# Second expansion of a two-block transformer kernel: 20 of 22 weight blocks by Strassen's scheme

## What is computed

```python
def swiglu(h, w_in, w_out):
    a, b = jnp.split(h @ w_in, 2, axis=-1)
    return (jax.nn.silu(a) * b) @ w_out

# in second_block, FFN_HIDDEN = 2816
h = rmsnorm(x, ffn_norm_pre[i]) * (1.0 + sc2) + sh2
y = swiglu(h, ffn_w_in[i], ffn_w_out[i])
x = x + g2 * rmsnorm(y, ffn_norm_post[i])
```

## Time and profile before

| | |
|---|---|
| median of 3 runs | 1345.88 us (1344.02 to 1346.18) |
| span of the profiled execution, first to last instruction | 1343.4 us |
| its own time | not listed; the runs' median is 2.5 us above the span |
| mean granted TensorE clock | 0.984 |
| busy: TensorE matmul | 1295.9 us, 96% |
| busy: weight loads | 1042.2 us, 78% |
| busy: VectorE, ScalarE, GpSimd | 544.9, 568.5, 591.2 us |
| chain that ended last, by engine | TensorE 85%, VectorE 6%, ScalarE 3%, DMA 3% |

### The profile page before, as it was taken

One profiled execution on the slowest core, in us unless ns is written; L12 is line 12 of the kernel. 1 busy time (PEld: TensorE's weight loads), 2 busy tenths in 40 slices (PEclk: granted clock), 3 DMA queues, 4 the chain that ended last, 5 costly groups with the idle time before them and its releaser, 6 DMA issues.

```text
span 1343.4 us, 17523 instructions
## 1 busy us (share of the span) xinstructions
PE 1295.9 (96%) x6464; PEld 1042.2 (78%) x6464; DVE 544.9 (41%) x1080; ACT 568.5 (42%) x938; POOL 591.2 (44%) x494
## 2 busy tenths in 40 slices
PE   7899999998989999999999899999899999999998
PEld 1688878677878888888888788667688888888886
DVE  2576652678436444443542352783520000001113
ACT  3713455767344322233323454785452323223232
POOL 0334332468043444444665733455224444445561
PEclk9999999999889999999999999899999999999999
DMA  9427557050243555554423411111202222222221
GB/s 393 179 77 270 187 172 142 1 189 1 73 178 125 199 200 196 187 187 157 157 94 99 162 64 69 56 30 61 91 32 97 98 105 105 95 94 94 94 94 63
DMA packets 27402, 166.77 MB, mean 124 GB/s; under 512 B 2976, under 2 KB 5280, under 8 KB 8656
## 3 DMA queue, kind: packets, MB, share of 16 engines
q1 hardware_dynamic: 25328, 151.31, 32.4%
q10 hardware_dynamic: 2016, 14.68, 2.9%
HBM read 163.85 MB, written 6.32 MB: 127 GB/s over the span
## 4 chain that ended last, share of the span: by engine, by line
PE 85%; DVE 6%; ACT 3%; DMA 3%; issue 1%; POOL 1%; SPq 0%; DVEq 0%; ACTq 0%
PE bank L275 55%; PE bank L334 12%; PE bank L311 6%; DMA ada_ring<-ada_dram 2%; DVE ada_ring L2018 1%; PE bank L1357 1%; PE bank L1329 1%; PE bank L714 1%; DMA w_raw<-w_dram 1%; PE bank L523 1%; DVE arena L2083 1%; PE bank L537 1%; PE bank L509 1%; PE bank L690 1%; POOL arena L942 1%
## 5 line engine op out<-in xcount | busy, mean ns | idle before, releaser
L268 POOL TENSOR_TENSOR w_lo<-w_raw,w_hi 128x512 fp32r<-128x512 f32 x328 | 444.0, 1385 | 620.2 <-ACT w_hi L259 620.2
L275 PE MATMUL bank<-h_hi,w_hi 128*128 128x512 f32 x1088 | 429.6, 395 | 7.4 <-DVE h_lo L450 4.5
L275 PE MATMUL bank<-h_lo,w_hi 128*128 128x512 f32 x1088 | 426.8, 392 | 0.0
L275 PE MATMUL bank<-h_hi,w_lo 128*128 128x512 f32 x1088 | 426.8, 392 | 0.0
L259 ACT ACTIVATE w_hi<-w_raw 128x2048 fp32r<-128x2048 f32 x86 | 164.8, 1917 | 309.0 <-PE bank L275 190.3
L275 PEld LDWEIGHTS bank<-h_hi,w_hi 128*128 128x128 f32 x1088 | 206.0, 189 | 51.4 <-issue 7.9
L275 PEld LDWEIGHTS bank<-h_hi,w_lo 128*128 128x128 f32 x1088 | 206.2, 190 | 43.5
L275 PEld LDWEIGHTS bank<-h_lo,w_hi 128*128 128x128 f32 x1088 | 206.4, 190 | 41.3
L2355 DVE TENSOR_TENSOR arena<-arena,bank 128x512 f32 (+1 forms) x22 | 15.1, 688 | 210.2 <-PE bank L275 210.2
L2211 DVE TENSOR_TENSOR h_lo<-arena,h_hi 128x1024 fp32r<-128x1024 f32 x22 | 32.4, 1485 | 135.1 <-ACT h_hi L1832 123.6
L2037 DVE SCALAR_TENSOR_TENSOR arena<-bank,params,arena 128x511 f32<-128x511 f32 (+1 forms) x36 | 25.3, 704 | 131.9 <-ACT arena L1807 111.6
(11 more groups left out here) (278 smaller groups left out, 1783.9 us busy)
## 6 DMA issues: line engine op xcount, KB each, us to landing
w_raw<-w_dram SPq DMA_DIRECT2D x92, 1024.0 KB, 4.7
ada_ring<-ada_dram SPq DMA_DIRECT2D x30, 1024.0 KB, 4.8
ada_ring<-ada_dram ACTq DMA_DIRECT2D x14, 1024.0 KB, 4.8
arena<-ada_dram SPq DMA_DIRECT2D x4, 1024.0 KB, 10.7
arena<-x_dram SPq DMA_DIRECT2D x2, 2048.0 KB, 11.5
bias_copies<-bias_rows SPq DMA_DIRECT2D x1, 4096.0 KB, 17.2
arena<-bias_copies SPq DMA_DIRECT2D x4, 768.0 KB, 5.7
ada_ring<-rpb_dram SPq DMA_DIRECT2D x16, 128.0 KB, 9.7
```

What stands on the lines that cost most here:

```text
L268: last = nc.gpsimd.tensor_tensor(w_lo[b % 2][:, part], w_raw[b % 2][:, part], w_hi[b % 2][:, part], ALU.subtract)
L275: last = nc.tensor.matmul(bank[:, :], w[:, ft, k, :], x[:, k, :], start=k == first and m == 0, stop=k == final and m == 2)
```

## The change

20 of the 22 expansion blocks, 61 to 80, are computed by Strassen's scheme in Winograd's form. A block is seen as a 2 x 2 matrix of quarters: inner dimension in halves of 4 chunks, output in gate and value tile. The activations are 2 x 2 as well: halves of the inner dimension by halves of the tokens (256 each). In place of 8 products of quarters there are 7, each 4 chunks x 3 matmuls with 256 moving columns, 84 matmuls in all.

- **Activation sums** (`h_sums`, four of 128x1024) are made once by VectorE after `h_lo`; ScalarE makes their high parts, VectorE two of the low parts and GpSimd two. `affine` keeps the full-precision activations in eight buffers (`h_full`).
- **Weight sums** (`w_sums`, four of 128x512) are made by VectorE for each block from `w_raw`.
- **Taking apart**: seven slots of 512 columns in the old `w_hi` and `w_lo` take the seven left operands. ScalarE makes seven copies of 512 columns (`high_slot`), GpSimd five subtractions and VectorE two (`low_slot`). A slot is refilled as soon as its product of the block before is done.
- **Putting together**: the seven products go to three banks (`PLACE`), two sets in turn. ScalarE copies products 0 and 4 out (`snapshot`), VectorE forms `left_gate` (512 columns), `third_sum`, `right_gate`, `left_value` (256 each, one input in a bank), GpSimd two 256-column sums from SBUF (`more_sums`). ScalarE's silu and VectorE's `gated2` now read SBUF alone.
- **Order**: TensorE's product 4 waits for the snapshot of product 0, product 5 for `third_sum`, product 6 for `left_gate`; a block waits for `gated2` of the block two before. The first contraction block is copied by ScalarE after product 3 of block 80 and is taken apart by GpSimd after `more_sums(19)`.
- The semaphores of the two attentions are merged and counted on by `of1`, which only renumbers waits.

```diff
+SEVEN0, SEVENS = B_UP2 + 2, 20
...
+        operand = [h_parts[0, 0], t_parts[1], h_parts[1, 0], t_parts[2], t_parts[0], h_parts[1, 1], t_parts[3]]
+        slot_part = [[w[1 - p // 4][:, p % 4 * 512:p % 4 * 512 + 512] for p in range(7)] for w in (w_hi, w_lo)]
+        seven_bank = [[ps[i] for i in (4, 5, 6)], [ps[i] for i in (1, 2, 3)]]
+        PLACE = [(0, 0), (1, 256), (1, 0), (2, 0), (0, 256), (2, 256), (1, 0)]
+        def slot_source(n, p):
+            return (raw_quarter(n, 0), w_sums[:, SUM2], raw_quarter(n, 1), w_sums[:, SUM3], w_sums[:, SUM1], w_sums[:, SUM4], raw_quarter(n, 3))[p]
...
@@ GpSimd
+            def low_slot(n, p, i=0):
+                pool.wait_ge(hi_done, HIGH0 + 7 * n + p + 1 + 14 * i)
+                nc.gpsimd.tensor_tensor(slot_part[1][p], slot_source(n, p), slot_part[0][p], ALU.subtract).then_inc(lo_done, 1)
+            def more_sums(n, i=0):
+                pool.wait_ge(seven_snap, 2 * n + 2 + 4 * i)
+                pool.wait_ge(seven_sum, 4 * n + 1 + 8 * i)
+                nc.gpsimd.tensor_tensor(u4[n % 2], gate_sum[n % 2][:, 256:512], p5_copy[n % 2], ALU.add).then_inc(seven_more, 1)
+                pool.wait_ge(seven_sum, 4 * n + 2 + 8 * i)
+                nc.gpsimd.tensor_tensor(value_sum[n % 2][:, 256:512], u3[n % 2], p5_copy[n % 2], ALU.add).then_inc(seven_more, 1)
+            def pool_turn(n, i=0):
+                for p in (0, 1, 2):
+                    low_slot(n + 1, p, i)
+                more_sums(n, i)
+                for p in (5, 6):
+                    low_slot(n + 1, p, i)
+            low_slot(0, 0)
+            low_slot(0, 1)
+            low_turned(2)
+            low_turned(0)
+            for p in (2, 5, 6):
+                low_slot(0, p)
...
@@ TensorE
+            def seven(n, i=0):
+                pe.wait_ge(tile_free, F_UP2 + 2 * n + 2 + 4 * i)
+                for p in range(7):
+                    if p in (3, 4):
+                        pe.wait_ge(seven_low, 2 + 2 * n + p - 2 + 4 * i)
+                    else:
+                        pe.wait_ge(lo_done, LOW0 + 5 * n + (p + 1 if p < 3 else p - 1) + 10 * i)
...
+                    if p == 4:
+                        pe.wait_ge(seven_snap, 2 * n + 1 + 4 * i)
+                    if p in (5, 6):
+                        pe.wait_ge(seven_sum, 4 * n + (2 if p == 5 else 1) + 8 * i)
+                    hi, lo = (slot_part[part][p].rearrange("p (k n) -> p k n", k=4) for part in range(2))
+                    out, (x_hi, x_lo) = product_at(n, p), operand[p]
+                    for k in range(4):
+                        for m, (w, x) in enumerate(((hi, x_hi), (hi, x_lo), (lo, x_hi))):
+                            last = nc.tensor.matmul(out, w[:, k], x[:, k], start=k == 0 and m == 0, stop=k == 3 and m == 2)
+                    last.then_inc(half_used, 1)
...
@@ ScalarE
+            def act_turn(n, i=0):
+                for p in range(7):
+                    if p == 0:
+                        snapshot(n, p, p1_copy, i)
+                    if p == 4:
+                        snapshot(n, p, p5_copy, i)
+                    if p == 6:
+                        gate_silu(n, i)
+                    high_slot(n + 1, p, i)
+            high_slot(0, 0)
+            for k, t in enumerate(TURNED):
+                act.wait_ge(t_sum, max(k, t) + 1)
+                nc.scalar.activation(t_parts[t][0], h_sums[:, t], ACT.Copy).then_inc(t_high, 1)
+            plain_silu(0)
...
+            act.wait_ge(half_used, USED0 + 7 * 19 + 4)
+            act.wait_ge(raw_in[1], 16 * (B_DOWN2 // 2 + 1))
+            nc.scalar.activation(w_hi[1][:], w_raw[1][:], ACT.Copy).then_inc(hi_done, 1)
+            snapshot(19, 4, p5_copy)
...
@@ VectorE
+            def weight_sums(n, i=0):
...
+                nc.vector.tensor_tensor(w_sums[:, SUM1], raw_quarter(n, 2), raw_quarter(n, 3), ALU.add).then_inc(w_sum, 1)
...
+                dve.wait_ge(w_sum, 4 * n + 1 + 8 * i)
+                nc.vector.tensor_tensor(w_sums[:, SUM2], w_sums[:, SUM1], raw_quarter(n, 0), ALU.subtract).then_inc(w_sum, 1)
+            def weight_sums_too(n, i=0):
+                nc.vector.tensor_tensor(w_sums[:, SUM3], raw_quarter(n, 0), raw_quarter(n, 2), ALU.subtract).then_inc(w_sum, 1)
...
+                nc.vector.tensor_tensor(w_sums[:, SUM4], raw_quarter(n, 1), w_sums[:, SUM2], ALU.subtract).then_inc(w_sum, 1)
...
+            def dve_turn(n, i=0):
+                if n:
+                    left_value(n - 1, i)
+                weight_sums(n + 1, i)
+                if n == 0:
+                    plain_gated(1)
+                else:
+                    gated2(n - 1, i)
+                weight_sums_too(n + 1, i)
+                left_gate(n, i)
+                third_sum(n, i)
+                low_slot(n + 1, 3, i)
+                low_slot(n + 1, 4, i)
+                right_gate(n, i)
```

More of the change, by code:

```diff
@@ L418, in spread, with affine @@
             return last
-        def affine(act, m, gain, shift, xn, hb, aside=None, turned=None):
+        def affine(act, m, gain, shift, xn, hb, aside=None, turned=None, slots=2):
             for c in range(DC):
@@ L429, in affine @@
                 nc.scalar.activation(h_hi[:, c, :], src, ACT.Identity, bias=shift(c), scale=gain(c))
[L430 removed]
+                if k >= 2 and slots == 2:
                     act.wait_ge(h_low, k - 1)
[L432 removed]
+                nc.scalar.activation(hb[:, c % slots, :], src, ACT.Identity, bias=shift(c),
                                      scale=gain(c)).then_inc(aff_done, 1)
@@ L1679, in _ @@
             lead_turned()
-            tiles(B_UP2 + 2, F_UP2 + 4, 9)
-            last_turn(B_UP2 + 20, F_UP2 + 40)
+            seven(0)
+            seven(1)
+            with pe.Fori(0, 9) as i:
+                seven(2, i)
+                seven(3, i)
             down_rows(B_DOWN2, 11, F_UP2 + 44)
@@ new lines, in plain_silu @@
+            def plain_silu(u):
+                act.wait_ge(half_used, 2 * B_UP2 + 2 * u + 1)
+                nc.scalar.activation(gate_sum[u], ps[2 * u][:, :], ACT.Silu).then_inc(tap_silu, 1)
+            high_slot(0, 0)
[3 more added lines that the diff above has]
+            plain_silu(0)
+            for p in (1, 2, 3):
+                high_slot(0, p)
@@ new lines, in _ @@
+            plain_silu(1)
+            for p in (4, 5, 6):
+                high_slot(0, p)
+            with act.Fori(0, 9) as i:
+                act_turn(0, i)
+                act_turn(1, i)
+            act_turn(18)
+            snapshot(19, 0, p1_copy)
+            for t in range(2):
+                nc.scalar.activation(h_hi[:, 2 * t:2 * t + 2, :], HID[:, 2 * t:2 * t + 2, :], ACT.Copy).then_inc(g_hi, 1)
+            act.wait_ge(half_used, USED0 + 7 * 19 + 4)
+            act.wait_ge(raw_in[1], 16 * (B_DOWN2 // 2 + 1))
@@ L2362, in _ @@
+            weight_sums(0)
+            turned_low(1)
+            weight_sums_too(0)
+            plain_gated(0)
+            turned_low(3)
+            low_slot(0, 3)
+            low_slot(0, 4)
+            dve_turn(0)
+            dve_turn(1)
+            with dve.Fori(0, 8) as i:
+                dve_turn(2, i)
+                dve_turn(3, i)
+            dve_turn(18)
+            left_value(18)
+            gated2(18)
             hidden_low(12, slice(0, 2), 0)
+            left_gate(19)
@@ L2363, in _ @@
+            third_sum(19)
             hidden_low(13, slice(2, 4), 2)
-            gated2(21)
+            right_gate(19)
+            left_value(19)
+            gated2(19)
             with dve.Fori(0, 3) as i:
```

198 lines of the change are left out of this document (149 added, 49 removed).

## The result

The kernel after takes 1407.39 us (median of 4 runs, 1406.23 to 1408.56), the one before 1345.81 (4 runs, 1344.02 to 1346.18): ratio 1.0463, 95% interval 1.0449 to 1.0478, 4.6% slower. The prediction was 1367.0, with a range of 1349 to 1382. The sign is right and the size is not: 61.6 us lost in place of 21.1. The profiled execution took 1407.43 us over a span of 1405.6, at a mean granted clock of 0.961.

A forecast was written before the change was run, and what follows sets the result against it. TensorE was taken to bound the kernel before, at 10.88 us a block. After: 19 x 11.6 = 220.4, + 2.5 + 15.1 + 0.7 = 238.7 us against 217.6, 21.1 slower; 1345.9 + 21.1 = 1367.0 us, range 1349 to 1382.

The forecast's parts named there:

- TensorE's own turn: 84 matmuls a block at 0.113 us, 9.52 us; as the bound it was a rival at 1325 us, chance 0.10.
- GpSimd and VectorE hold each other up: Two-SBUF-input VectorE operations and GpSimd's exclude each other: floor 10.9 us a turn; as the bound a rival, 1354 us, 0.18.
- The rival by which a VectorE operation is paid for whole: Both engines hold SBUF for their full duration, 0.69 in place of 0.45 us: turn 12.5, 1384 us, chance 0.08.
- VectorE's chain: Part of the turn from left_value through the weight sums, gated2 and left_gate to the end of third_sum.
- the good case: Second weight sum 0.7 us after the first, not 1.7 as when GpSimd gets between: turn 11.1 rather than 12.1 us.
- Products 5 and 6: TensorE's part of the turn, both products and the end of the last matmul, before left_value: 2.9 us.
- the sum of the turn: Walk from product 5's start through VectorE's operations to third_sum's end: 11.1 or 12.1 us, middle 11.6 taken.
- its last rival: The clock falls: TensorE's 2 us pauses put a third of the turns at 1.2 GHz, 1384 us, chance 0.06.
- the start: First Strassen block, slots freed as block 60 ends and GpSimd's second slot late: 2.5 us, between 0 and 5.
- the walk: At the start, GpSimd's second slot ready at 1004.2 us, where product 2 would start at 1002.6.
- the collision: One GpSimd meeting with VectorE before the contraction, within the 15.1 us from the last block's start.
- The clock's share of that pause: Lower clock from TensorE's 5.5 us stand before the contraction: 0.7 us taken, 1.7 in the cited rows.

The follow-up runs named there:

- the versions with banks: Kernel after with first and second weight sum written to idle PSUM banks, slots 1 and 3 swapped between VectorE and GpSimd, sums ahead of gated2: 1329.59 us.
- with one SBUF input: Kernel after with the second SBUF input of VectorE's seven two-input operations read from an idle bank from block 62, values wrong: 1334.81 us.
- the reordered version: Kernel after with the third and fourth weight sum made after third_sum, nothing else changed: 1351.79 us, ratio 1.0062 to the kernel before.
- the versions with fillers: Kernel after with useless 256-column matmuls ahead of TensorE's wait for product 5: 1380.07 us with 18, 1382.15 us with 9.
- the end mended: Version with weight sums in banks, plus the contraction's first block copied and taken apart quarter by quarter as products finish: 1324.32 us.

## Why the prediction was right in sign and wrong in size

- **What bounds the turn: right.** TensorE waits before product 5, released by `third_sum`, once in every turn; a block's own matmuls are no longer the bound.
- **TensorE's own turn: 9.52 us put, 9.76 measured** where nothing hinders it (the versions with banks and with one SBUF input). The spacing is 0.113 to 0.120 us, 0.116 on average, where line 1357 had 0.113.
- **GpSimd and VectorE hold each other up: right.** 0.45 us for a VectorE operation gave a floor of 10.9 us, and the reordered version runs at 10.85 with both engines full. The narrow GpSimd sum was put at 0.76 us and takes 0.75. The rival by which a VectorE operation is paid for whole would have put the floor at 7.77 + 7 x 0.69 = 12.6 us; it is out.
- **VectorE's chain: 8.65 us put (the middle of 8.15 and 9.15), 8.9 measured.** The second weight sum does follow the first after 0.71 us, the good case. But the fourth sum waits for a GpSimd operation in hand as the others do: from its issue to `left_gate` 1.69 us, where I had 0.6. With 9.09 in the versions with fillers, 0.25 to 0.45 us a turn were missing.
- **Products 5 and 6: 2.9 us put, 4.73 measured. This is the step that failed.** At full clock the same part takes 3.17 us (0.3 more than put, from the spacing and the way from the last matmul to VectorE). The rest, 1.56 us, is the lower clock; the sum of the turn put it at nothing. A turn without it is 1.40 us shorter, as VectorE's chain then grows by 0.16. The prediction had the mechanism as its last rival, at 0.06, with both products at half speed in a third of the turns: 1384 us. The runs show it in every turn, with 16.7 of the two products' 24 matmuls.
- **Why it was put aside.** I set against it: 90.8 of 100 us busy and a clock of 0.94. That row averages over 100 us with pauses of all lengths; it does not say what one pause of 2 us does if it comes again in every turn. The other rows of the same group were nearer: the clock fell behind a stretch with 2.82 of 8 us busy, but that stretch held longer pauses. Neither has this pattern, so the honest bounds for the clock ran from no turn to every turn. Every turn, with products 5 and 6 at twice 2.7 us, would have been 19 x 2.7 = 51 us on top: an upper end near 1418 in place of 1382. The range was too narrow on this term. The Trainium skill (TensorE: Matmul & The Clock Gate, Part 1) has the clock fall to half behind an idle stretch; the trace agrees on the level (0.213 us a matmul against 0.117), and adds that the pauses of this turn are enough.
- **The ends: near.** Block 80's first matmul comes 262.3 us after block 61's; less 19 turns of 13.65 that leaves 2.9 us for the start, put at 2.5. The size is in part luck: product 2 came 2.9 us late, where the walk had 1.6, and 2.5 was the middle of 0 to 5. From block 80's start to the contraction it is 15.0 us, put at 15.1 (the terms as listed, with 0.45 for the collision, add up to 15.0). The clock's share of that pause was put at 0.7 us, though the rows cited for it gave 1.7, and is 2.6: it falls in the first matmuls of the contraction.
- **The sum.** Turns 19 x 2.05 = 39.0, start +0.4, last block and its clock -0.8: the 38.6 us by which the 277.3 exceed my 238.7. With 2.6 in the contraction that is 41.2, against 40.5 between the forecast and the median; the profiled executions are 0.6 us further apart than the medians. Of the 2.05 us a turn 1.40 are the clock, shown by the fillers, and 0.65 the chain and the two products at full clock (12.25 against 11.6). One range does not follow from its terms: turns of 11.2 to 11.9 with 0 to 5 us at the start give 1357 to 1375, where the forecast has 1358 to 1376. Nothing hangs on it.

**Where the gain went.** Seven products in place of eight save 10.88 - 9.76 = 1.12 us a block, 22 us in all. The weight sums put seven VectorE operations with two SBUF inputs beside seven GpSimd ones, and the pair needs 10.85 us: the gain is gone. The order puts another 1.4 us on the chain (12.25), and the pause that this leaves on TensorE another 1.4 by the clock (13.65). With two sums in banks the gain is back but for the ends, 1329.6 us; with the end mended it is 1324.3, 20 us faster than before and close to the 22 us that the products save.

## What to carry to other kernels

When work moves from a saturated TensorE to VectorE and GpSimd, count VectorE operations with both inputs in SBUF separately, for each costs GpSimd more time than the sums show; an idle PSUM bank as the place of one input takes the cost away. Where a dependency leaves a pause in every turn, price the clock from the pause and its recurrence, with every turn as the upper end, and look whether the products behind it are on the chain. Such a pause can be tested cheaply: a few useless matmuls in front of the wait tell the clock from the wait.

## What the runs showed of the hardware

- A pause of 2.3 us (from start to start) in each turn of 13.65, with TensorE busy for 84% of the time, put 16.7 of 84 matmuls at the lower clock level, in every turn. A pause of 1.1 to 1.4 us in turns of 10.85 to 12.25 left one long spacing a turn, the first behind the pause.
- A single pause of 5 us before the contraction slowed the next thirteen or fourteen 512-column matmuls in the kernel after and in the version with banks: they are 0.427 us apart in place of 0.227, and it cost 2.6 and 2.9 us against the 125.95 of the kernel before. The same pause of 5.07 us slowed only seven of them and cost 1.4 us in the reordered version, so its length does not fix its price. First the kernel after, then the reordered version, ten microseconds from the contraction's start:

```profile
1277.00:1287.00 10.00, 9.98 (x33) 8.03 (x34) 0.00 (x0) 0.00 (x0) 4.80 (x4) 0.73 0.61 210
...
1221.30:1231.30 10.00, 10.00 (x39) 8.17 (x40) 0.00 (x0) 0.00 (x0) 4.75 (x4) 0.86 0.58 211
```

- In strict alternation of 512-column operations the pair advances every 1.69 to 1.71 us, 1.25 of GpSimd's and 0.45 of VectorE's: an operation of 0.68 us by itself holds the other up for two thirds of its time.
- Writing to a bank does not take the exclusion away, reading an input from one does: the first weight sum, to bank 7 from two SBUF inputs, lasts 847 ns on average, the second and fourth, with one input in a bank, 699 and 686. GpSimd's subtraction, issued while the first sum runs, takes 1.62 us, where an undisturbed one in the same turn takes 1.29:

```profile
1106.87 0.84 DVE L2531 TENSOR_TENSOR bank<-w_raw 128x512 f32<-128x512 f32 x1
1107.75 0.70 DVE L2535 TENSOR_TENSOR bank<-bank,w_raw 128x512 f32<-128x512 f32 x1
...
1107.24 1.62 POOL L1377 TENSOR_TENSOR w_lo<-w_raw,w_hi 128x512 fp32r<-128x512 f32 x1
```
